# A two-layer encoder trunk on one core: attention by look-ahead, pooling maps by the half bank, and the output projection begun inside attention

## The chip, the cores and the metric

The kernel runs on one core of one Trainium2 chip. The time is the device time of one execution, in microseconds (us). The engines are PE (TensorE, matmuls and transposes), DVE (VectorE), ACT (ScalarE), POOL (GpSimd) and SP (SyncE, which here only issues DMAs). Each works through its own instructions in order and waits on semaphores for the others.

## The reference

Two layers over 528 tokens (16 meta tokens and 512 others) of width 1024, all in float32. Cut to what matters:

```python
for l in range(DEPTH):
    xn = rms_norm(h, attn_norm_g[l])
    q, k, v, u = jnp.split(xn @ w_in[l], splits, axis=-1)     # 512, 128, 128, 512 columns
    q = apply_rope(rms_norm(q, q_norm_g[l]), cos, sin) * q_scale
    k = apply_rope(rms_norm(k, k_norm_g[l]), cos, sin)
    attn = sliding_sink_attention(q, k, v, sinks[l])
    pool = multiscale_pool(u, w_pool[l], pool_scale[l])
    h = h + jnp.concatenate([attn, pool], axis=-1) @ w_out[l]
    xn = rms_norm(h, ffn_norm_g[l])
    g = causal_dwconv(xn @ w_gate[l], conv_w[l], conv_b[l])
    h = h + (gelu(g) * (xn @ w_up[l])) @ w_down[l]
```

There are 8 query heads and 2 key heads of 64. Attention goes by chunks of 64 queries; each sees the 16 meta tokens and its own and the previous chunk, with a learned sink in the softmax. The pooling mixer has four groups of 128 channels: the trailing mean over 2, 4, 8 or 16 positions less the token, and then a 128x128 map per group.

## The kernel before

Activations lie with features on the 128 partitions and the 528 tokens along the free dimension; a tile of the projection is 128 features by 528 tokens. PSUM holds it as a slot of two banks with 264 tokens in each (`slot[0..3]`). Every float32 product is made of three matmuls of rounded parts: weights high by activations high, high by low, low by high. So a tile over 1024 input features is 8 x 3 x 2 = 48 matmuls of 264 columns. ACT makes the high part of a weight block (`split_hi`, L391) and DVE the low part (`split_lo`, L404). A weight unit is 256 columns, and units take turns in two buffers; SP loads one when the low split of its predecessor in the buffer is done.

A layer's first half goes, on PE:

- the tiles k, v, the mean square of the features for the norm (its inverse root `rinv` is applied when a tile is evacuated), q0, the transposes of v, k's mean square, q1, q2, the means of q0 and q1 (`q_means`), q3, u3, five rows of the filling, the means of q2 and q3;
- eleven steps of attention. There are nine blocks b of queries (`NB`). Step s has `scores(s)`, `heads(s - 2)` and `probs_T(s - 1)` (the transposes of the probabilities). DVE in step s copies and evacuates `heads_lo(s - 3)`, divides block s - 1 by its sums (`divide`), takes the maxima of block s (`row_maxima`); ACT takes the exponentials of block s (`exps`), and copies;
- between them the filling (`project_side`): the pooling tiles u2, u1, u0 in half tiles of 264 tokens, in the one half bank that attention leaves free (`side`, in slot 3). One row is one input block: three matmuls. `SIDE_ENDS` says how many rows each step has in front of it in all. The half bank is free again when DVE's `u_half` has read it;
- the four pooling maps (`pool_map`, six matmuls each), over two banks of a slot of the scores, in the steps `MAP_AT`;
- the output projection, eight tiles of 48 matmuls, from the step after the last.

Rotary embedding is on three engines: DVE multiplies by the sines (`sine_part`), ACT shifts that by half a head (`shift`), POOL multiplies by the cosines and adds (`rotated`). POOL also makes the running sums of the pooling (`group`).

The order on each engine is written out by hand: the loop over steps stands once in each engine's block, with numbers of steps for what joins it. Each of the waits is a count of a semaphore: `filled[s]` and `evac[s]` for slot s (s = 4 is the side half bank), `hi_split` and `lo_split` for the weights, `meta_out` for DVE's copy of the meta probabilities, on which `heads` waits. In `split_hi` the count goes up only with the second half:

```python
            ins = nc.scalar.activation(w_hi[s][:, a:b], raw[s][:, a:b], ACT.Copy)
            if b == nk:
                ins.then_inc(hi_split[s], 1)
```

The MLP (from 177.3 us in layer 0 and 714.4 in layer 1) is computed in three chunks, with a fast scheme of seven products for the down projection. It has the same code before and after.

## Time and profile before

| | |
|---|---|
| median of 3 executions | 1091.09 us (1089.04 to 1093.24) |
| the profiled execution | 1094.96 us, span of its instructions 1093.2 us, granted clock 0.982 |
| PE busy | 1045.8 us (96%), 7932 matmuls |
| DVE busy | 738.5 us (68%) |
| ACT busy | 475.7 us (44%) |
| POOL busy | 107.7 us (10%) |
| HBM | 91.65 MB read, 86 GB/s over the span |

The ends of matmuls are modelled, and a busy PE is not PE at its peak: a matmul's row shows 280 ns at full clock while the next begins 120 ns after it. Busy time says little about the stages; what counts is when the first matmul of a stage starts, and what PE waited for. The first half of layer 0 lasts from 15.23 to 177.30 us, that of layer 1 from 561.66 to 714.45. The stages in them are: projections to 74.9 (615.6), steps to 129.3 (668.1), output projection.

### The profile page before, as it was taken

What the parts mean: (1) busy time and instruction counts of PE and PEld (TensorE: products, weight loads), DVE (VectorE), ACT (ScalarE), POOL (GpSimd) and SP (SyncE); (2) the same over time, 40 slices, a digit from 0 to 9 for tenths busy, and PEclk for the clock granted to TensorE, in tenths of its full rate; (3) what the DMA queues carried; (4) which work ended last, traced back from release to release, by engine and by line L of the source; (5) the groups of instructions that cost most, each with busy time, mean ns of one, the idle gap of its engine ahead of it and who ended that gap; (6) DMA issues with size and microseconds to landing.
All of it is one profiled execution on the core that took longest, in us unless ns stands there. A gap on an engine that the chain in (4) does not pass through costs nothing.

```text
span 1093.2 us, 19011 instructions
## 1 busy us (share of the span) xinstructions
PE 1045.8 (96%) x7932; PEld 999.3 (91%) x7932; DVE 738.5 (68%) x1134; ACT 475.7 (44%) x714; POOL 107.7 (10%) x109
## 2 busy tenths in 40 slices
PE   7899899999999999999899988999999999999997
PEld 6797799999999999999899977999989999899987
DVE  5566644568955689557886576546698466975686
ACT  5675534434413344134347755354343333423341
POOL 1262000000000000000002610001000000000000
PEclk9899899999999999999999999999999999999999
DMA  7211132232232322321231112332313332233112
GB/s 207 98 49 39 52 104 77 78 100 80 93 116 78 101 80 92 117 78 58 94 106 53 49 40 78 98 96 77 115 40 117 116 114 80 77 118 112 62 58 78
DMA packets 93566, 94.99 MB, mean 87 GB/s; under 512 B 3392, under 2 KB 91800, under 8 KB 93480
## 3 DMA queue, kind: packets, MB, share of 16 engines
q1 hardware_dynamic: 92768, 93.01, 26.5%
q8 instruction: 63, 1.03, 0.4%
q0 software_dynamic: 400, 0.58, 0.2%
q10 hardware_dynamic: 312, 0.18, 0.1%
q14 instruction: 23, 0.19, 0.1%
HBM read 91.65 MB, written 2.10 MB: 86 GB/s over the span
## 4 chain that ended last, share of the span: by engine, by line
PE 74%; DVE 12%; ACT 8%; issue 4%; DMA 1%; SPq 0%; POOL 0%; DVEq 0%; ACTq 0%; POOLq 0%
PE slot L552 57%; PE slot L787 14%; ACT probs L1065 3%; DVE h L1550 2%; ACT w_hi L400 1%; DVE nmax L1360 1%; DMA x_in<-in_x 1%; ACT rot_s L990 1%; DVE ms_work L1311 1%; DVE probs L1379 1%; DMA cst<-const_table 1%; ACT m_op_hi L1158 1%; DVE w_lo L411 1%; DVE mix_lo L1395 0%; ACT x_hi L917 0%
## 5 line engine op out<-in xcount | busy, mean ns | idle before, releaser
L552 PE MATMUL slot<-x_hi,w_hi 128*128 128x264 f32 (+2 forms) x1552 | 362.8, 301 | 7.0 <-DVE u_sb L1342 3.9
L552 PE MATMUL slot<-x_lo,w_hi 128*128 128x264 f32 (+2 forms) x1552 | 359.4, 299 | 0.0
L552 PE MATMUL slot<-x_hi,w_lo 128*128 128x264 f32 (+2 forms) x1552 | 359.0, 299 | 0.0
L552 PEld LDWEIGHTS slot<-x_hi,w_hi 128*128 128x128 f32 x1552 | 253.7, 190 | 19.6 <-DVE u_sb L1342 5.3
L552 PEld LDWEIGHTS slot<-x_lo,w_hi 128*128 128x128 f32 x1552 | 252.1, 190 | 7.3
L552 PEld LDWEIGHTS slot<-x_hi,w_lo 128*128 128x128 f32 x1552 | 251.9, 190 | 7.5
L411 DVE TENSOR_TENSOR w_lo<-raw,w_hi 128x2048 fp32r<-128x2048 f32 (+1 forms) x63 | 145.5, 2309 | 90.5 <-ACT w_hi L400 90.5
L400 ACT ACTIVATE w_hi<-raw 128x2048 fp32r<-128x2048 f32 (+2 forms) x65 | 118.3, 1820 | 145.2 <-PE slot L552 89.8
L903 POOL TENSOR_TENSOR work<-work 128x528 f32<-128x528 f32 (+1 forms) x32 | 41.9, 1309 | 714.0 <-DVE work L1481 350.6
L787 PE MATMUL slot<-m_op_hi,w_hi 128*128 128x264 f32 (+1 forms) x352 | 103.4, 294 | 8.3 <-DVE m_op_lo L1514 4.8
L787 PE MATMUL slot<-m_op_hi,w_lo 128*128 128x264 f32 (+1 forms) x352 | 100.9, 287 | 0.0
L787 PE MATMUL slot<-m_op_lo,w_hi 128*128 128x264 f32 (+1 forms) x352 | 100.9, 287 | 0.0
L1550 DVE TENSOR_TENSOR h<-slot,h 128x264 f32<-128x264 f32 (+1 forms) x192 | 79.5, 425 | 28.0 <-PE slot L787 24.1
L1135 ACT ACTIVATE work<-gate,par_all 128x528 f32<-128x528 f32 (+1 forms) x44 | 31.9, 731 | 118.6 <-DVE gate L1268 59.8
L438 ACT ACTIVATE w_hi<-w_sum 128x1024 fp32r<-128x1024 f32 (+1 forms) x48 | 47.4, 987 | 79.3 <-DVE w_sum L1532 60.7
L787 PEld LDWEIGHTS slot<-m_op_hi,w_hi 128*128 128x128 f32 x352 | 67.7, 192 | 12.5 <-DVE m_op_lo L1514 6.0
L787 PE MATMUL slot<-m_op_hi,w_ext_hi 128*128 128x264 f32 (+1 forms) x264 | 75.6, 286 | 1.8 <-DVE m_op_lo L1514 1.8
L787 PE MATMUL slot<-m_op_hi,w_ext_lo 128*128 128x264 f32 (+1 forms) x264 | 75.1, 285 | 0.0
L787 PE MATMUL slot<-m_op_lo,w_ext_hi 128*128 128x264 f32 (+1 forms) x264 | 75.0, 284 | 0.0
L787 PEld LDWEIGHTS slot<-m_op_lo,w_hi 128*128 128x128 f32 x352 | 67.8, 193 | 0.0
L787 PEld LDWEIGHTS slot<-m_op_hi,w_lo 128*128 128x128 f32 x352 | 67.8, 193 | 0.0
L1141 ACT ACTIVATE work<-work,par_all 128x528 f32<-128x528 f32 (+1 forms) x44 | 31.8, 730 | 70.6 <-DVE work L1472 70.4
(163 smaller groups left out, 1502.4 us busy)
## 6 DMA issues: line engine op xcount, KB each, us to landing
raw<-in_w_gate SPq DMA_DIRECT2D x44, 512.0 KB, 4.7
raw<-in_w_up SPq DMA_DIRECT2D x44, 512.0 KB, 4.6
raw<-in_w_down SPq DMA_DIRECT2D x32, 512.0 KB, 4.4
raw<-in_w_in SPq DMA_DIRECT2D x19, 512.0 KB, 5.0
raw<-in_w_out SPq DMA_DIRECT2D x16, 512.0 KB, 4.4
raw<-in_w_down SPq DMA_DIRECT2D x16, 384.0 KB, 3.6
x_in<-in_x SPq DMA_DIRECT2D x4, 512.0 KB, 6.3
out<-y_out SPq DMA_DIRECT2D x8, 256.0 KB, 2.9
```

Of the source, the lines that this page charges most:

```text
L400: ins = nc.scalar.activation(w_hi[s][:, a:b], raw[s][:, a:b], ACT.Copy)
L411: ins = nc.vector.tensor_tensor(w_lo[s][:, a:b], raw[s][:, a:b], w_hi[s][:, a:b].bitcast(f32), ALU.subtract)
L438: nc.scalar.activation(dst, src, ACT.Copy).then_inc(opnd_hi[n], 1)
L552: ins = nc.tensor.matmul(out_part, w[ws][:, r, cols], a[:, k, tokens], start=first and n == 0 and w is w_hi and a is a_hi, stop=end and w ...
L787: ins = nc.tensor.matmul(dst, part[s][w][:, wn, kk], m_op[a][:, m, kk, 0:width], start=first and kk == kks[0] and n == 0 and name in ("P1" ...
L903: nc.gpsimd.tensor_tensor(up[c][:, t0:], up[c][:, t0:], conv[c][:, t0:], ALU.mult)\
L990: ins = nc.scalar.activation(rot_s[to:to + 32], sine[fr:fr + 32], ACT.Copy)
L1065: ins = nc.scalar.activation(probs[:, y, t, 0:nk], slot[s][:, t // 2, col], ACT.Exp, bias=nm[:, y, t:t + 1], scale=q_scale[:, b, t // 2, t ...
L1135: nc.scalar.activation(conv[c][:, t0:], gate[c][:, 2 + t0:], ACT.Copy, scale=par[:, tap:tap + 1])\
L1141: nc.scalar.activation(conv[c][:, t0:], conv[c][:, t0:], ACT.Gelu, bias=par[:, bias:bias + 1])\
L1158: nc.scalar.activation(m_op[0][:, 3:7, kk, 0:width], m_sum[:, :, 0:width], ACT.Copy)\
L1550: nc.vector.tensor_tensor(rows, bank, rows, ALU.add).then_inc(h_added, 1)
```

## The change

- **Look-ahead.** `scores` and `row_maxima` run one step ahead of `exps`: PE makes `scores(s + 1)` and DVE `row_maxima(s + 1)` in step s. `scores(0)` and `row_maxima(0)` stand in front of the steps. The copy of the meta probabilities goes from the end of DVE's step to the head of the next.
- **Order of the tiles.** The units of w_in are cut anew (k with q3's columns, and so on, with the queries' tiles in reverse). k, norm, q0, k's mean, q1, q2, means, q3, u3, u0, means, `scores(0)`, and then v, whose transposes are in step 1. u3 and u0 are whole tiles in front; u2 and u1 are the filling, 32 rows in steps 1 to 4.
- **Maps.** One map in each of the steps 5 to 8, in two halves of three matmuls through the side half bank; ACT and DVE evacuate each half (264 columns) in place of 528.
- **Output projection.** `out_rows` makes the four pooling rows of tile out0 in step 9 and of out1 in step 10; the attention rows follow by halves of the tokens. Splits of w_out are made in halves in steps 6 to 11.
- **Rotary.** `sine`, `rot_c` and `rot_s` are doubled, in memory of v_T and of the running sums, so that a stage waits for the tile before last.
- **First norm of layer 0.** Row sums of squares come from ACT (`accum_out`) on x before its transposes, with a root and a reciprocal of [128, 5]; five small matmuls spread them over the partitions. The layer's squares, their sums, the logarithm and the exponential go. ACT copies the result to `rinv` and loads the table of roots at the start.
- **Constants.** The table of sines, cosines and counts is loaded by SP, after the first weights, and no longer by POOL after the sinks.

The diff, cut to its core:

```diff
@@ Psum: order of the slots
-            order += [(f"scores{b}", 1 - b % 2)] + {5: [("pool3", 1)], 8: [("pool2", 0), ("pool1", 0)]}.get(b, [])
+        order += [(f"scores{b}", b % 2) for b in range(NB)]
+        order += [(f"{name}{half}", 4) for name in ("u2", "u1", "pool3", "pool0", "pool2", "pool1") for half in "ab"]
...
-            sine = v_T[:]
+            sine = [v_T[:], run_b[:, PAD:]]
+            rot_c = [sb(sc, f"rot_c{n}", [P, L])[:] for n in range(2)]
+            rot_s = [sb(sc, "rot_s", [P, L])[:], run_a[:, PAD:]]
...
-        GROUPS = (3, 2, 1, 0)
-        SIDE_ENDS = [5, 8, 14, 20, 26, 32, 38, 44, 48, 48, 48, 48, 48]
-        POOLED_AT, POOL_HI_AT, POOL_LO_AT, MAP_AT = (1, 4, 6, 9), (2, 5, 7, 9), (3, 6, 9, 9), (5, 8, 9, 10)
+        GROUPS = (3, 0, 2, 1)
+        SIDE_ENDS = [0, 0, 8, 16, 24, 32, 32, 32, 32, 32, 32, 32, 32]
+        POOLED_AT, POOL_HI_AT, POOL_LO_AT, MAP_AT = (0, 1, 4, 5), (1, 2, 6, 7), (2, 3, 6, 7), (5, 6, 7, 8)
...
@@ PE
-                for step in range(NB + 2):
-                    if step < NB:
-                        scores(step)
+                scores(0)
+                project("v", U_VU0)
+                for step in range(NB + 2):
+                    if step == 1:
+                        v_transposed()
...
+                    project_side(first, cut)
+                    if step + 1 < NB:
+                        scores(step + 1)
+                    if step == NB:
+                        open_slot("out0", l)
+                        pe.wait_ge(lo_split[U_OUT % 2], slot_turn(l, U_OUT) + 2)
+                        out_rows(0, (7, 4, 6), first=True)
+                    if step == NB + 1:
+                        open_slot("out1", l)
+                        out_rows(1, (7, 4, 6, 5), first=True)
                     if step >= 2:
                         heads(step - 2)
+                    if step in MAP_AT:
+                        pool_map(MAP_AT.index(step), 0)
+                    if step == NB:
+                        out_rows(0, (5,))
                     if 1 <= step <= NB:
                         probs_T(step - 1)
+                    if step in MAP_AT:
+                        pool_map(MAP_AT.index(step), 1)
                     project_side(cut, end)
...
@@ ACT
+                act.wait_ge(x_loaded[t], 16)
+                nc.scalar.activation(y_out[:, t], x_in[:, t], ACT.Square, accum_out=row_ms[:, t:t + 1])\
+                  .then_inc(row_summed, 1)
...
-            for k in range(KT):
-                square(0, 0, k)
...
+                    if step in MAP_AT:
+                        for half in range(2):
+                            pool_map_hi(MAP_AT.index(step), half)
+                    if step in POOL_HI_AT:
+                        pooled_hi(POOL_HI_AT.index(step))
+                    if step in (6, 7):
+                        split_hi(act, l, U_OUT, half=step - 6)
+                    if step in (9, 10):
+                        split_hi(act, l, U_OUT + 1, half=step - 9)
@@ DVE
                     if 3 <= step < NB + 2:
                         meta_probs_out(step - 2)
                     if step >= 3:
                         heads_lo(step - 3)
                     if 1 <= step <= NB:
                         divide(step - 1)
-                    if step < NB:
-                        row_maxima(step)
+                    if step + 1 < NB:
+                        row_maxima(step + 1)
                     if side_done(step) is not None:
                         u_half(side_done(step))
+                    if step in MAP_AT:
+                        for half in range(2):
+                            pool_map_lo(MAP_AT.index(step), half)
+                    if step in (7, 8):
+                        split_lo(dve, l, U_OUT, half=step - 7)
+                    if step in (9, 11):
+                        split_lo(dve, l, U_OUT + 1, half=step // 2 - 4)
```

PE's order at a map, in layer 0. Before (step 5 with the third pooling group's map over both banks of slot 1; `pool_hi` is the pooled tile, `x_hi` the filling, `k_win` the scores, `v_meta` the heads, `probs_pad` the transposes):

```order
L669 MATMUL slot0<-k_win,q_rot 128x144 x3
L552 MATMUL slot1<-pool_hi,w_hi1 128x264 [waits plo_ready,lo_split1,evac1]
L552 MATMUL slot1<-pool_hi,w_hi1 128x264
L552 MATMUL slot1<-pool_lo,w_hi1 128x264 x2
L552 MATMUL slot1<-pool_hi,w_lo1 128x264 x2
L552 MATMUL slot3<-x_hi,w_hi0 128x264 [waits evac4]
```

and after, the same step:

```order
L697 MATMUL slot0<-k_win,q_rot 128x144 x3
L724 MATMUL slot3<-probs_meta,v_meta 128x128 [waits meta_out,evac2,evac3]
L724 MATMUL slot3<-probs_meta,v_meta 128x128
L731 MATMUL slot3<-probs_win,v_win 64x128 x4
L569 MATMUL slot3<-pool_hi,w_hi1 128x264 [waits plo_ready,lo_split1,evac4]
L569 MATMUL slot3<-pool_lo,w_hi1 128x264
L569 MATMUL slot3<-pool_hi,w_lo1 128x264
L709 MATMUL slot2<-cst,probs_pad 128x128 [waits probs_ready,meta_out,evac2]
L712 MATMUL slot2<-cst,probs 128x128 x4
L569 MATMUL slot3<-pool_hi,w_hi1 128x264 [waits plo_ready,evac4]
L569 MATMUL slot3<-pool_lo,w_hi1 128x264
L569 MATMUL slot3<-pool_hi,w_lo1 128x264
```

The map went from one group of six, with its own slot and filling behind it, to two groups of three in the half bank, the second of which waits for `evac4`, the evacuation of the first.

DVE's order behind the row maxima of layer 0. Before, in step 6 (`u_sb` is the evacuation of the half bank):

```order
L1365 TENSOR_TENSOR sink_arg<-nm,sink_all 128x4 [waits dve_attn]
L1342 TENSOR_TENSOR u_sb<-slot3,rinv 128x264 [waits filled4,pooled_ready]
L1294 SCALAR_TENSOR_TENSOR pooled<-run_a,u_sb 128x528 [waits plo_ready,run_ready]
L1300 TENSOR_TENSOR pool_lo<-pooled,pool_hi 128x528 [waits phi_ready]
L1388 COPY probs_meta<-slot2 128x128 [waits filled2]
L1395 TENSOR_TENSOR mix_lo<-slot3,mix_hi 128x4x64 [waits mixhi_ready]
```

and after, in step 7 (`mix_lo` from `par_all` is a map's half, `w_lo0` the first half of the low split of w_out):

```order
L1416 TENSOR_TENSOR sink_arg<-nm,sink_all 128x4 [waits dve_attn]
L1400 SCALAR_TENSOR_TENSOR mix_lo<-slot3,par_all,mix_hi 128x264 [waits mixhi_ready] x2
L1352 TENSOR_TENSOR pool_lo<-pooled,pool_hi 128x528 [waits phi_ready]
L421 TENSOR_TENSOR w_lo0<-raw0,w_hi0 128x1024 [waits hi_split0]
L1439 COPY probs_meta<-slot2 128x128 [waits filled2]
L1446 TENSOR_TENSOR mix_lo<-slot3,mix_hi 128x4x64 [waits mixhi_ready]
```

Both halves of the map and the split now stand ahead of the copy and the heads' `mix_lo`, which PE's next heads wait for (`meta_out`, `evac3`).

## Rows read from the trace of the kernel before

**Rows 1.** windows: length, busy us (x) of PE PEld DVE ACT POOL, PEclk, DMA

```profile
15.20:74.90 59.70, 54.33 (x403) 53.31 (x404) 37.26 (x39) 44.40 (x68) 20.00 (x22) 0.91 0.27 82
74.90:97.80 22.90, 20.84 (x167) 18.13 (x167) 15.38 (x47) 11.76 (x47) 7.99 (x9) 0.93 0.04 12
97.80:129.30 31.50, 25.35 (x202) 20.86 (x202) 24.06 (x62) 20.02 (x65) 3.96 (x5) 0.93 0.12 38
129.30:177.30 48.00, 48.00 (x387) 48.00 (x385) 21.80 (x23) 16.49 (x19) 0.00 (x0) 0.97 0.34 108
561.70:615.60 53.90, 51.94 (x404) 50.86 (x403) 33.19 (x33) 37.62 (x56) 18.73 (x19) 0.97 0.26 83
638.00:668.10 30.10, 23.95 (x203) 19.54 (x202) 23.75 (x62) 20.03 (x65) 3.97 (x5) 1.00 0.11 36
668.10:714.40 46.30, 46.30 (x384) 46.30 (x385) 21.94 (x24) 16.49 (x19) 0.00 (x0) 1.00 0.36 114
```

**Rows 2.** waits of PE: who waited for whom, us in total, times, longest us

```profile
PE slot L696 <- DVE mix_lo L1395: 6.5, 8, 1.2
PE slot L621 <- DVE v_T L1268: 4.6, 2, 3.9
...
PE slot L552 <- DVE u_sb L1342: 3.9, 6, 1.1
```

**Rows 3.** windows over three stretches at half clock

```profile
15.90:19.30 3.40, 3.40 (x18) 3.40 (x17) 3.40 (x6) 3.40 (x6) 0.60 (x1) 0.50 0.06 0
39.80:46.60 6.80, 5.85 (x23) 5.39 (x24) 2.12 (x4) 5.70 (x12) 1.30 (x1) 0.50 0.40 139
125.10:131.90 6.80, 6.26 (x30) 5.71 (x31) 3.87 (x5) 2.71 (x3) 0.00 (x0) 0.50 0.46 152
```

**Rows 4.** timeline of PE: start us, us, operation, count, [idle before <-releaser]

```profile
57.00 2.07 PE L607 MATMUL slot<-cst,head_sq 128*128 128x2 f32 x18
...
95.81 0.29 PE L552 MATMUL slot<-x_hi,w_lo 128*128 128x264 f32 x1
95.93 0.61 PE L696 MATMUL slot<-probs_meta,v_meta 128*128 128x128 f32 x4
...
97.06 0.33 PE L681 MATMUL slot<-cst,probs_pad 128*128 128x128 f32 x1
...
97.75 0.76 PE L669 MATMUL slot<-k_win,q_rot 64*128 64x144 f32 x8
```

**Rows 5.** timeline of DVE, a split in front and a step of attention

```profile
19.75 1.22 DVE L1242 TENSOR_TENSOR w_lo<-raw,w_hi 128x1024 fp32r<-128x1024 f32 x1
...
94.50 0.42 DVE L1395 TENSOR_TENSOR mix_lo<-slot,mix_hi 128x256 fp32r<-128x256 f32 x1 [1.71 <-ACT mix_hi L1086]
94.84 0.15 DVE L1371 TENSOR_TENSOR den<-row_sum,sink_exp 128x4 f32<-128x4 f32 x1
...
95.99 0.75 DVE L1360 TENSOR_REDUCE nmax<-slot 128x4 f32<-128x576 f32 x1
...
97.25 0.43 DVE L1342 TENSOR_TENSOR u_sb<-slot,rinv 128x264 f32<-128x264 f32 x1
```

**Rows 6.** waits of ACT before 16 us

```profile
ACT h L939 <- PE slot L586: 4.5, 4, 2.1
```

**Rows 7.** timeline of ACT

```profile
18.41 1.04 ACT L947 ACTIVATE w_hi<-raw 128x1024 fp32r<-128x1024 f32 x1
...
33.36 1.92 ACT L400 ACTIVATE w_hi<-raw 128x2048 fp32r<-128x2048 f32 x1 [4.62 <-DMA cst<-const_table]
35.30 1.28 ACT L963 ACT_TABLE_LOAD   x1
...
99.27 0.38 ACT L1086 ACTIVATE mix_hi<-slot 128x256 fp32r<-128x256 f32 x1
```

**Rows 8.** timeline of POOL and DVE at 88 us

```profile
88.20 1.07 POOL L884 TENSOR_TENSOR run_a<-run_b 128x528 f32<-128x528 f32 x1
...
88.36 0.93 DVE L1371 TENSOR_TENSOR den<-row_sum,sink_exp 128x4 f32<-128x4 f32 x1
```

More of the change, by code:

```diff
@@ L530, in open_slot, with dense @@
                 return s
-            def dense(s, ws, col, rows, a_hi, a_lo, first=True, last=True, ready=None, part=None, real=False, tail=False):
+            def dense(s, ws, col, rows, a_hi, a_lo, first=True, last=True, ready=None, part=None, real=False, tail=False,
+                      parts=(0, 1)):
                 if real:
@@ L622, in _ @@
-                nc.tensor.transpose(flat[0:N_META, NWIN * P:(NWIN + 1) * P], v_T[:, 0:N_META], ident)\
-                  .then_inc(filled[s], 1)
+                project("k", U_KQ3, ready=lambda k: pe.wait_ge(xlo_ready, l * (2 * KT) + (k + 1)))
+                if l > 0:
+                    column_mean("attn_norm", l, all_mean, sumsq, *norm_added(l, 0, KT - 1))
+                else:
+                    s = open_slot("attn_norm", 0)
+                    pe.wait_ge(row_inv, 1)
+                    for t, (bank, c0, n) in enumerate(ROW_TILES):
+                        ins = nc.tensor.matmul(slot[s][:, bank, c0:c0 + n], row_ms[0:n, t:t + 1].broadcast_to([n, P]),
+                                               ident[0:n, 0:n], start=True, stop=True)
+                    ins.then_inc(filled[s], 1)
@@ new lines, in _, with v_transposed @@
+                project("u3", U_Q0U3)
+                project("u0", U_VU0)
+                q_means(1)
+                def v_transposed():
+                    s = open_slot("v_T", l)
+                    pe.wait_ge(evac[ps.slot("v")], ps.before("v", l) + 1)
+                    flat = slot[s][:].rearrange("p a t -> p (a t)")
+                    for w in range(NWIN):
+                        t0 = N_META + w * CHUNK
+                        nc.tensor.transpose(flat[:, w * P:(w + 1) * P], v_T[:, t0:t0 + P], ident)
+                    nc.tensor.transpose(flat[0:N_META, NWIN * P:(NWIN + 1) * P], v_T[:, 0:N_META], ident)\
+                      .then_inc(filled[s], 1)
@@ L706, in heads @@
                     ins.then_inc(filled[s], 1)
-                name = "heads0"
-                pe.wait_ge(evac[ps.slot(name)], ps.before(name, l))
-                project_side(*side_rows(-1))
-                q_means(1)
-                for step in range(NB + 2):
-                    if step < NB:
-                        scores(step)
-                    for n in (0, 1):
-                        if step == MAP_AT[n]:
-                            pool_map(n)
-                    first, end = side_rows(step)
-                    done = side_done(step)
-                    cut = (first + end) // 2 if done is None else (done + 1) * KT
-                    project_side(first, min(cut, end))
+                last_layer = l + 1 == DEPTH
@@ new lines, in out_rows @@
+                def out_rows(t, ks, first=False, last=False, parts=(0, 1)):
+                    s, unit = ps.slot(f"out{t}"), U_OUT + t // 2
+                    for k in ks:
+                        if k >= 4:
+                            name = f"pool{k - 4}b"
+                            pe.wait_ge(evac[4], ps.before(name, l) + 1)
+                    return dense(s, unit % 2, (t % 2) * P, [(k, k) for k in ks], mix_hi, mix_lo, first=first, last=last,
+                                 tail=last_layer, parts=parts)
@@ L749, in _ @@
-                for t in range(KT):
-                    s, unit = open_slot(f"out{t}", l), U_OUT + t // 2
+                for t in range(2):
+                    out_rows(t, (0, 1, 2, 3), last=True, parts=(0,))
+                name = f"heads{NB - 1}"
+                pe.wait_ge(evac[ps.slot(name)], ps.before(name, l) + 1)
+                for t in range(2):
+                    out_rows(t, (0, 1, 2, 3), last=True, parts=(1,)).then_inc(filled[ps.slot(f"out{t}")], 1)
+                for t in range(2, KT):
+                    s, unit = open_slot(f"out{t}", l), U_OUT + t // 2
+                    if t == 2:
+                        pe.wait_ge(meta_out, l * (NB - 1) + (NB - 1))
@@ L751, in _ @@
                     if t % 2 == 0:
                         pe.wait_ge(lo_split[unit % 2], slot_turn(l, unit) + 2)
-                    dense(s, unit % 2, (t % 2) * P, rows, mix_hi, mix_lo, ready=mixed if t == 0 else None,
-                          tail=l + 1 == DEPTH).then_inc(filled[s], 1)
+                    out_rows(t, (7, 4, 6, 5, 0, 1, 2, 3), first=True, last=True).then_inc(filled[s], 1)
                 def mlp_tiles(i):
@@ L1304, in _ @@
                 scaled("k", k_dup[:, 0])
-                scaled("v", v_T[:])
                 q_tile(0)
                 dve.wait_ge(qtab_ready, l + 1)
-                dve.wait_ge(evac[ps.slot("v_T")], ps.before("v_T", l) + 1)
                 sine_part(0)
```

347 lines of the change are left out of this document (166 added, 181 removed).

## The prediction

> **What bounds the kernel now.** I read the windows by stage first [rows 1]. TensorE (PE) is busy almost throughout, and the out projection shows its bare speed: 384 matmuls of 264 columns in 48.0 us, less the slow clock at its start, 0.122 us each, so 48 of them (a tile) take 5.86 us, and with the switch of operand ahead of it about 5.96. The attention block of a layer, from the first scores to the out projection, takes 54.4 us in layer 0 (22.9 and 31.5) and 52.5 in layer 1. Its matmuls, by the spacing of one step [rows 4] (heads 1.13, transposes of the probabilities 0.69, scores 0.7), are 43 side rows of three (15.7), four maps (2.9), scores 6.1, heads 9.5, transposes 5.6, together 39.8 us; so 13 to 15 us in each layer are waits and slow clock. The list of PE's waits [rows 2] names what ends them: mix_lo (the evacuation of the heads' bank), u_sb (of the side half bank), and ahead of attention v_T, 3.9 us of it in layer 0. Third, the granted clock: after the wait on v_T it was half for 6.8 us (0.50, that is 1.2 GHz), as at the very start for 3.4 us, and again at the end of layer 0's steps [rows 3]. Fourth, one step of attention on PE, DVE and ACT [rows 4, 5]: PE goes from heads to the next scores in 1.8 us and then has the side rows or a map; DVE works in strict order: heads' low part, division, row maxima, side half bank, and what else the step has.
>
> **Front of layer 0.** Five squares with a row sum join ACT ahead of the copies of h, each about 1.1 us (1024 columns took 1.04), 5.5 us; ACT waited 4.5 us for PE there, so 1.1 us come late, with the small root [rows 6]. The first matmul goes from 15.2 to 16.3. In return eight squares, seven sums, and two table loads of 1.28 leave the path to rinv, and so does ACT's wait for the constant table (4.6 us of waiting at 33.4) [rows 7]. From there PE: seven tiles (k, four q, u3, u0) 41.7, norm 1.1, k's mean square 0.7, two means of q 2.0 each [rows 4], 1.7 for the slow clock at the start, and a new wait of 1.1: k's squares follow, on ACT and DVE, the copies of rinv, a split of 1.9, one of 2.3 and k_dup. Sum 50.3: the first scores come at 66.6. Before: 59.7 us with 5 side rows (1.8) and the transposes of v (0.9) more, so 57.0 against 50.3, a gain of 6.7, less 1.1 for the late start. The double rot_c, rot_s and sine take POOL and ACT off each other's way, but no longer wait of PE names them in the old trace [rows 2]: nothing, and the least of it is shown by the 2 us by which my places for the low splits lie ahead of the tiles that need them. The const load stands on SP's queue behind the first weights and in front of the next ones; those land 1.5 us later and are used 8 us later: nothing.
>
> **Front of layer 1.** The old order has 53.9 us, the wait on v_T and one on head_sq in it; the same work less 5 side rows and v's transposes would be 51.2. The new: seven tiles 41.7, about 0.5 for x_lo's pace, norm 0.7, k's mean 0.7, means of q 4.0, sum 47.6, so the scores start at 609.3. Gain 3.6.
>
> **Steps 0 to 4.** v's tile fills the time in which the first scores go through DVE and ACT: 0.55 and 5.96. Then scores 0.7, 0.25 waiting for v_T, transposes 0.9, four steps with 8 side rows (2.93 and 0.2 for switches) 12.5, scores 2.8, heads 2.8, transposes 2.2. Between two half tiles PE waits for u_sb: the last matmul's 0.28, DVE 0.43 [rows 4, 5], 0.13 to restart, less the usual spacing, 0.74, three times 2.2. Sum 24.3; v done at 73.1, the side rows at 97.4 (layer 1: 640.1). The exponentials do leave the loop, as the order shows: row maxima run a step ahead. In units of the old work this part is 1.4 us quicker in layer 0, about 1 in layer 1.
>
> **Steps 5 to 8** carry the loss. Side rows are gone, and each step has one map in two halves through one half bank, in the order heads, map a, transposes, map b; DVE takes both evacuations one after the other, and only after them, at the head of the next step, the copy of the meta probabilities and mix_lo, on which PE's heads wait. From the start D of DVE's step: copy 0.2, mix_lo 0.34 and 0.08, PE restarts at 0.75, heads to 1.88, map a to 2.35, drained 2.51; ACT's half 0.40 (256 columns took 0.38 [rows 7]) to 2.95; DVE is then just through with the division (1.15) and the maxima (1.26); its half 0.42 to 3.4; map b 3.6 to 4.2 drained; ACT 4.66; DVE 5.07. Then a pooled tile 0.61 (step 5), or ACT's 0.65 and DVE's 0.61 (step 6): periods 5.7 and 5.85 for 3.6 us of PE work. Step 7: ACT's half split of w_out (1.04) in step 6 delays its heads by 0.5, and at its end DVE's first half of the low split waits for ACT's second half, since the semaphore is counted only at the whole: 7.85. Step 8: 5.07 and another half split of 1.22 [rows 5], and PE opens out0 at 6.4. D5 is at 99.15 (97.4, then u_sb, pooled, split), D6 105.65, D7 111.5, D8 119.35. One collision with POOL is in D6: the last tile's adds run in step 5, and DVE's 4-column sum took 0.93 instead of 0.15 beside such an add [rows 8]; 0.8.
>
> The Trainium skill (SBUF — State Buffer, section Who interferes with whom) says that a VectorE instruction with two SBUF inputs is blocked for the whole of a GpSimd instruction that reads SBUF. The rows agree for one add: both ended at 89.3. By the rule both adds of the last tile can block one DVE instruction each, 2.1 us in place of 0.8, which would make the time 2.6 us longer in the two layers.
>
> Step 9 and 10: eight rows of out0 and out1 (5.86 and switches 0.3) stand between the last heads, 7 to 10 us of work that was behind them. DVE's half split in step 9 waits for ACT's step 10 and costs 0.6 ahead of heads8, done at D8 + 16.25 = 135.6. The remaining out rows take 41.1: end at 176.7, before 177.3. Layer 1: 640.1 + 38.2 + 40.2 = 718.6 (the last layer's tiles are narrower), before 714.4.
>
> **Clock.** In step 7 to 8 PE stands for 4.0 us, and waits of 1.5 to 2.4 stand in each step. In the old trace a wait of 3.9 was followed by 6.8 us at half clock, and smaller ones, 0.8 to 1.2 each, by 6.8 us at the end of layer 0 and by none in layer 1 [rows 1, 3]. A stretch of 3.4 us costs up to 1.7. No such stretch per layer is one end and three the other, 0 to 5.1 us; I take 2.5, one and a half of them, nearest to the row of the 3.9 us wait (two, with much of the first spent idle).
>
> **Sum.** −0.6 and +4.2 and 2 × 2.5 = +8.6 us. MLP, load sizes and the end are unchanged. The profiled execution (span 1093.2, time 1094.96) would be 1103.5; it is 3.9 above the median of 1091.09, so the median becomes 1099.6.
>
> **Rivals.** (A) *Faster, 1084, chance 0.20*: the half-bank trips of steps 5 to 8 fit beside PE's other work. I price the late stretch 7 us a layer above the old one in like work (38.2 with 6.1 of out rows, against 31.5 with 5.9 of side rows); if it costs no more than before, the sum without clock is +3.6 − 14 = −10, with some clock −7. It decides when PE's waits in steps 5 to 8 fall below 7 us a layer; I work out 14. For it: half of them hang on ACT's and DVE's order being as tight as I add it. Against: the waits on mix_lo are there today, with fewer trips.
> (B) *No change, 1093, chance 0.27*: the clock holds through the steps and POOL does not collide: 3.6 − 1.6 = +2. For it: layer 1 of the old kernel had no slow stretch in these steps.
> (C) *The head start doesn't come, 1106, chance 0.07*: the sinks, landed at 26 us before, land later; ACT now waits for them (through DVE's preparation) ahead of k's squares. Seven us later and layer 0's gain is gone.
> The forecast: 0.46.
>
> A difference under 0.5% (5.5 us) is about what this measurement can't tell from none. Faster than that: A, 0.20. Within: B with 0.27 and 0.03 of the forecast's own low side, 0.30. Slower: 0.43 and C, 0.50. Range 1083 to 1107; the forecast's own, by the clock's bounds (−5 to +5.2) and 2.6 of POOL, 1094 to 1107.
>
> **What would show it.** Right: first matmul near 16.3, no wait on v_T above 0.5, scores0 at 66 to 67; PE waits on mix_lo of 1.5 to 2.5 in four steps and 4.0 in one, one on w_lo near 2 ahead of out0; half clock at step 8; layer 0's out projection ends at 177 to 180, layer 1's stage grows from 152.8 to 157 to 160 us. Wrong: periods of steps 5 to 8 under 5 us, or a front of layer 0 that is not 5 us shorter.

## The result, and the profile after

The changed kernel takes 1111.5 us, median of 4 runs (1108.3 to 1113.6), against 1090.5 (1089.0 to 1093.2) of the kernel before: ratio 1.0187, 95% interval 1.0164 to 1.0210. It is slower, as forecast, but by 21 us where I had 8.6, and outside the range of 1083 to 1107. Its profiled execution took 1111.45 us with a span of 1109.7, 16.5 more than the span before.

The windows by stage of the changed kernel, in the columns of [rows 1]: the front, first scores to the filling's end, then to the end of the last heads, the out projection; in layer 1 the front, steps 5 to the last heads, out projection; and two stretches at half clock:

```profile
17.95:67.86 49.91, 49.15 (x387) 48.67 (x387) 33.68 (x31) 31.05 (x49) 24.61 (x25) 0.97 0.24 70
67.86:100.25 32.39, 30.32 (x245) 27.52 (x244) 20.04 (x53) 19.50 (x68) 5.58 (x6) 0.95 0.11 34
100.25:144.68 44.43, 31.32 (x194) 25.54 (x193) 24.33 (x61) 19.60 (x57) 3.13 (x3) 0.77 0.15 48
144.68:185.65 40.97, 40.97 (x339) 40.97 (x337) 20.29 (x23) 14.37 (x18) 0.00 (x0) 1.00 0.32 104
568.41:616.12 47.71, 47.33 (x382) 46.63 (x380) 34.09 (x32) 34.07 (x49) 23.55 (x23) 1.00 0.25 73
647.02:690.87 43.85, 30.22 (x194) 24.72 (x194) 24.32 (x61) 19.60 (x57) 3.13 (x3) 0.81 0.15 49
690.87:731.55 40.68, 40.68 (x338) 40.68 (x337) 20.21 (x23) 14.38 (x18) 0.00 (x0) 1.00 0.32 104
124.30:131.10 6.80, 5.07 (x23) 4.07 (x23) 3.21 (x8) 3.01 (x12) 0.00 (x0) 0.50 0.00 0
670.40:677.20 6.80, 4.90 (x22) 3.95 (x23) 3.33 (x8) 3.17 (x13) 0.00 (x0) 0.50 0.00 0
```

In layer 0 the front is 49.9 us where it was 59.7 [rows 1], or 57.0 in like work; the filling's end to the last heads takes 44.4, and in layer 1 43.9, where the prediction had 38.2. Of these 44 us PE is busy for 31, and its mean clock is 0.77 and 0.81. The rest of the out projection takes 41.0 and 40.7, close to the forecast of 41.1 and 40.2. PE's waits (us in total, times, longest), to be held against [rows 2]:

```profile
PE slot L724 <- DVE mix_lo L1446: 14.5, 8, 3.8
...
PE slot L569 <- issue: 4.6, 2, 2.3
PE slot L724 <- ACT probs_win L1131: 4.3, 2, 2.2
...
PE slot L655 <- DVE v_T L1318: 0.7, 2, 0.4
```

The wait on mix_lo ahead of the heads went from 6.5 to 14.5 us with one of 3.8; that on v_T, 3.9 before, is two of 0.36. "issue" is the wait for out0's weights, 2.3 us a layer. How a step comes to its wait is seen at the head of step 7 of layer 1. ACT first:

```profile
660.72 0.48 ACT L1058 ACTIVATE mix_hi<-slot,par_all 128x264 fp32r<-128x264 f32 x1 [1.35 <-PE slot L569]
661.10 0.63 ACT L1053 ACTIVATE pool_hi<-pooled 128x528 fp32r<-128x528 f32 x1
661.63 1.04 ACT L410 ACTIVATE w_hi<-raw 128x1024 fp32r<-128x1024 f32 x1
662.58 0.37 ACT L1141 ACTIVATE mix_hi<-slot 128x256 fp32r<-128x256 f32 x1
662.85 0.59 ACT L1131 ACTIVATE probs_win<-slot 128x512 f32<-128x512 f32 x1
```

then DVE, and PE, whose heads wait at 661.4 (scores behind half b, and the idle time in brackets):

```profile
661.24 0.49 DVE L1400 SCALAR_TENSOR_TENSOR mix_lo<-slot,par_all,mix_hi 128x264 fp32r<-128x264 f32 x1 [1.34 <-ACT mix_hi L1058]
661.77 0.71 DVE L1352 TENSOR_TENSOR pool_lo<-pooled,pool_hi 128x528 fp32r<-128x528 f32 x1
662.39 0.28 DVE L1439 COPY probs_meta<-slot 128x128 f32<-128x128 f32 x1
662.99 0.42 DVE L1446 TENSOR_TENSOR mix_lo<-slot,mix_hi 128x256 fp32r<-128x256 f32 x1 [0.31 <-ACT mix_hi L1141]
```

```profile
660.61 0.76 PE L697 MATMUL slot<-k_win,q_rot 64*128 64x144 f32 x8
663.54 1.15 PE L724 MATMUL slot<-probs_meta,v_meta 128*128 128x128 f32 x4 [2.16 <-ACT probs_win L1131]
```

The heads of the step before had been finished at 657.8, yet ACT touches them (L1141) at 662.58: ahead stand half b of step 6's map (660.72), which PE makes only after half a was read out, the pooled tile and a half split. DVE's copy of the meta probabilities (L1439) and mix_lo (L1446) stand behind the same half b, and PE's new heads wait 2.16 us for both engines.

One side term can be read at once. POOL's last sum runs in step 5 of layer 0; POOL, and the two instructions of DVE that end with its two adds:

```profile
101.55 1.38 POOL L923 TENSOR_TENSOR run_b<-u_sb 128x528 f32<-128x528 f32 x1 [8.89 <-DVE pooled L1346]
103.01 1.07 POOL L923 TENSOR_TENSOR run_a<-run_b 128x528 f32<-128x528 f32 x1
```

```profile
102.46 0.49 DVE L1422 TENSOR_TENSOR den<-row_sum,sink_exp 128x4 f32<-128x4 f32 x1
...
103.20 0.96 DVE L1426 TENSOR_TENSOR probs_pad<-probs,rden 128x64 f32<-128x64 f32 x1
```

They take 0.49 and 0.96 where they take 0.15 ([rows 5]) and 0.23 (at 656.39 us in the next step of layer 1) elsewhere: 1.07 us together, and the same in layer 1. The prediction had 0.8 a layer from one collision [rows 8]. The Trainium skill (SBUF — State Buffer, section Who interferes with whom) was right that both adds hold one DVE instruction each; the 2.1 us that I had worked out from it for that are twice the measured cost. Each instruction is held only for what is left of its add when it begins, 0.47 us of the first and 0.88 of the second, and would itself have taken 0.15 and 0.23 of that.

### The profile page after: what moved, and what is told of

The parts are those of the page before. It is cut to its first block, busy times and chain, and to the rows that moved or that the text cites. A ratio compares the mean times of both kernels' runs of the same rounds, so it can differ in the third digit from the quotient of the medians.

```text
span 1109.7 us, 19066 instructions
## 1 busy us (share of the span) xinstructions
PE 1050.9 (95%) x7938; PEld 1002.0 (90%) x7938; DVE 743.3 (67%) x1139; ACT 474.8 (43%) x725; POOL 111.3 (10%) x108
## 4 chain that ended last, share of the span: by engine, by line
PE 84%; DVE 8%; issue 4%; ACT 2%; DMA 1%; SPq 0%; DVEq 0%; ACTq 0%
PE slot L569 65%; PE slot L826 14%; DVE h L1600 2%; PE slot L724 1%; PE slot L731 1%; DMA x_in<-in_x 1%; DVE w_lo L421 1%; ACT w_hi L410 1%; PE slot L623 1%; PE slot L712 1%; PE slot L697 1%; ACT m_op_hi L1209 1%; DVE w_sum L1580 0%; PE slot L579 0%; DVE x_lo L1277 0%
## 5 line engine op out<-in xcount | busy, mean ns | idle before, releaser
L569 PE MATMUL slot<-x_hi,w_hi 128*128 128x264 f32 (+2 forms) x1552 | 357.9, 299 | 6.6 <-DVE u_sb L1394 3.4
L569 PE MATMUL slot<-x_lo,w_hi 128*128 128x264 f32 (+2 forms) x1552 | 355.4, 298 | 0.0
L569 PE MATMUL slot<-x_hi,w_lo 128*128 128x264 f32 (+2 forms) x1552 | 355.3, 298 | 0.0
L569 PEld LDWEIGHTS slot<-x_lo,w_hi 128*128 128x128 f32 x1552 | 249.6, 189 | 7.3
L421 DVE TENSOR_TENSOR w_lo<-raw,w_hi 128x2048 fp32r<-128x2048 f32 (+2 forms) x67 | 148.2, 2212 | 94.1 <-ACT w_hi L410 94.1
L1186 ACT ACTIVATE work<-gate,par_all 128x528 f32<-128x528 f32 (+1 forms) x44 | 31.9, 730 | 118.7 <-DVE gate L1318 59.9
L826 PEld LDWEIGHTS slot<-m_op_hi,w_hi 128*128 128x128 f32 x352 | 66.2, 188 | 14.5 <-issue 7.6
```

Source lines behind the costliest of these rows:

```text
L421: ins = nc.vector.tensor_tensor(w_lo[s][:, a:b], raw[s][:, a:b], w_hi[s][:, a:b].bitcast(f32), ALU.subtract)
L569: ins = nc.tensor.matmul(out_part, w[ws][:, r, cols], a[:, k, tokens], start=first and n == 0 and w is w_hi and a is a_hi, stop=end and w ...
L826: ins = nc.tensor.matmul(dst, part[s][w][:, wn, kk], m_op[a][:, m, kk, 0:width], start=first and kk == kks[0] and n == 0 and name in ("P1" ...
L1186: nc.scalar.activation(conv[c][:, t0:], gate[c][:, 2 + t0:], ACT.Copy, scale=par[:, tap:tap + 1])\
```

## The experiments

In each pair of numbers the first is layer 0. "Late stretch" is from the end of the filling to the end of the last heads. Ratios are to the kernel before, which ran beside each.

**e1: PE kept busy in its waits.** In the changed kernel:

```diff
+                FILLER = {5: 10, 6: 10, 7: 14, 8: 26, 9: 16}
...
+                        filler(FILLER.get(step, 0), open_slot(f"scores{step + 1}", l))
                         scores(step + 1)
+                    if step == NB - 1:
+                        filler(FILLER.get(step, 0), open_slot("out0", l))
                     if step == NB:
-                        open_slot("out0", l)
+                        filler(FILLER.get(step, 0), open_slot("out0", l))
```

`filler(n, s)` issues n matmuls of x_hi by x_hi, 264 columns, into the slot just opened, which the next real matmul overwrites.

> The changed kernel with 76 more matmuls a layer whose result is thrown away, of 264 columns each, put into the waits of PE that its trace shows (10, 10, 14, 26 and 16 of them in steps 5 to 9, ahead of the scores or of out0). No other instruction changes. Theory CLOCK (the 17 to 20 us a layer at half clock make the stretch from the filling's end to heads8, 44.4 and 43.9 us, longer than the 38.2 worked out at full clock): the granted clock stays at 1.0 there, both stretches shrink to 38.5 to 40 us, and the time falls by 8 to 11 us, ratio 0.990 to 0.993. Rival STRUCTURE (the waits on ACT and DVE set the periods and the slow clock only fills what would be waits): clock at 1.0 as well, but stretches within 1 us of 44, ratio 1.000.

Measured: 1101.5 us (1.0099, 1.0077 to 1.0122), 10 us less than the changed kernel. The late stretches (windows):

```profile
100.71:139.22 38.51, 32.85 (x271) 28.31 (x269) 24.31 (x61) 19.69 (x57) 3.13 (x3) 1.00 0.17 56
643.62:682.09 38.47, 32.86 (x271) 28.29 (x270) 24.30 (x61) 19.68 (x57) 3.13 (x3) 1.00 0.17 56
```

38.5 and 38.5 us at full clock, against 38.2 worked out. So the structure was priced right within 0.3 us a layer, and the half clock cost 5.9 and 5.4 us a layer there: theory CLOCK. More work on PE made the kernel faster.

**e2: half b read out late.** ACT and DVE serve the next step's heads first:

```diff
 # ACT                                     # DVE in the same way, with meta_probs_out, heads_lo, pool_map_lo
                     if 2 <= step < NB + 2:
                         probs_out(step - 2)
+                    if step - 1 in MAP_AT:
+                        pool_map_hi(MAP_AT.index(step - 1), 1)
                     if step < NB:
                         exps(step)
                     if step in MAP_AT:
-                        for half in range(2):
-                            pool_map_hi(MAP_AT.index(step), half)
+                        pool_map_hi(MAP_AT.index(step), 0)
```

> The changed kernel with the second half of each map read out later: ACT and DVE first do the next step's copies and low part of the heads, and then half b of the map. PE's order is the same. Theory TRIPS (heads wait because both halves of a map stand ahead of the copy of the meta probabilities and of mix_lo): PE's waits on mix_lo in steps 6 to 9, 1.6, 2.2, 3.8 and 2.3 us, shrink by 1.5 to 2 us each, the stretch from the filling's end to heads8 goes from 44 to 36 to 39 us, the clock has fewer slow windows, time 12 to 18 us shorter, ratio 0.984 to 0.989. Rival CHAIN (exponentials, division and transposes set the period): under 3 us in all, ratio above 0.997.

Measured: 1091.2 us (1.0004, 0.9989 to 1.0020): the whole of the 20 us is back, more than I expected. The late stretches:

```profile
98.15:130.00 31.85, 23.71 (x194) 19.16 (x193) 23.67 (x61) 19.37 (x57) 3.13 (x3) 1.00 0.21 67
634.56:668.37 33.81, 26.55 (x194) 21.75 (x194) 23.73 (x61) 19.47 (x57) 3.14 (x3) 0.90 0.19 63
```

31.9 us at full clock in layer 0 (and 6.8 us at half clock in layer 1's): 6.6 less than e1 has. ACT at the same place as above:

```profile
645.80 0.38 ACT L1141 ACTIVATE mix_hi<-slot 128x256 fp32r<-128x256 f32 x1
646.06 0.60 ACT L1131 ACTIVATE probs_win<-slot 128x512 f32<-128x512 f32 x1
646.54 0.49 ACT L1058 ACTIVATE mix_hi<-slot,par_all 128x264 fp32r<-128x264 f32 x1
```

The high part of the heads and probs_win now come ahead of half b (646.54), and of the waits of 1.6 and 2.2 us ahead of the heads of steps 6 and 7 nothing is left; of the 3.8 in step 8, 1.65 is left, and the 1.58 of step 5 stays. The two late stretches are 12.6 and 10.0 us shorter than in the changed kernel, and 6.7 and 4.7 shorter than in e1. So about half of the gain is the order itself, and the other half is half clock that doesn't come up any more. Theory TRIPS, though "trips" is not the right word, as e9 shows.

**e3: DVE's half split counted by itself** (a semaphore `half_split` that ACT's first half raises, and DVE's first half waits for in place of `hi_split`).

> The changed kernel with one more semaphore: ACT counts the first half of its split of w_out, and DVE's first half waits for that alone. Theory SPLIT WAIT (DVE's half split in step 7 waits for ACT's second half ahead of the heads, and in step 9 for that of step 10): 0.2 to 0.5 us a layer in step 7, where the trace of the changed kernel shows only 0.24 us of DVE waiting, and 0 to 0.6 in step 9; time 0.5 to 2 us shorter, ratio 0.998 to 0.9995. Rival, as the prediction had it (7.85 against 5.85 us for step 7, the split wait its larger part): 2 us a layer, ratio 0.996.

Measured: 1109.8 us (1.0175, 1.0150 to 1.0199), 1.7 us off. The runs spread from 1107.8 to 1112.0, those of the changed kernel from 1108.3 to 1113.6, so a small gain can't be told from none; the rival's 4 us are at the edge of the interval. In the prediction's step 7 the wait was meant to cost more. That step's 7.85 us held all the same: at full clock, in e1, DVE's copies of the meta probabilities of steps 7 and 8 of layer 1 start at 658.12 and 666.01, 7.89 us apart. What is in them besides the wait, the split itself and ACT's, was not separated.

**e4: no head start.** `out_rows` of steps 9 and 10 and the half splits go; ACT splits w_out at step 9, DVE at step 10, the rows follow the steps.

> The changed kernel without the output projection in steps 9 and 10 and without the half splits of w_out in steps 6 to 11: the splits are whole, at step 9 (ACT) and 10 (DVE) and after the steps, and all rows of out0 and out1 follow the steps. Theory TRIPS: DVE and ACT lose 1.2 and 1.0 us in each of the steps 6 to 8, so the stretch to heads8 shrinks by 3 for these and by 7 for the rows of out0 and out1 that are made later, while the rows come after it with a wait for the splits of 2 to 4 us: time within 3 us of the changed kernel. Rival HEAD START PAYS: steps 9 and 10 stand empty for about 6 us a layer, 8 to 12 us slower, ratio above 1.007.

Measured: 1111.5 us (1.0190, 1.0167 to 1.0212), no change, as TRIPS had it. But one of its windows shows what else is in it:

```profile
114.50:138.40 23.90, 18.69 (x85) 14.66 (x86) 11.72 (x31) 12.59 (x31) 0.00 (x0) 0.50 0.05 13
```

23.9 us in one piece at half clock in layer 0's late steps. Without the rows of out0 and out1 in them these steps keep PE less busy, so the comparison holds the clock too; e11 makes it again.

**e5: late half b, the semaphore of e3, and 24 fillers a layer** (10 in step 5, 10 in step 8, 4 in step 9).

> The kernel with half b read out late, with the half split's own semaphore, and with 24 thrown-away matmuls a layer in the waits of PE that its trace still shows (10 in step 5, 10 in step 8, 4 in step 9). The run of half b late had 3.4 and 10.2 us at half clock in the two layers' steps and took 1091.2. Theory CLOCK: with the filling the second layer's 6.8 us at half clock in steps 8 and 9 go, and its steps, 65.0 us from the first scores, come down to the first layer's 63.0; with 0.5 to 1 us a layer from the semaphore the time is 1087 to 1089, ratio to the kernel before 0.997 to 0.999. Rival STRUCTURE: nothing but the semaphore's part, 1089.5 to 1091.

Measured: 1086.8 us (0.9973, 0.9960 to 0.9985), below both kernels. No half clock is left in the steps of layer 0, and in layer 1 only 3.4 us right behind the first scores. This is read from the trace of an execution of 1084.85 us, 2.0 under the median.

**e6: ACT's part of e2 alone** (DVE still reads half b ahead of the copy and mix_lo).

> The changed kernel with ACT's part of the late reading alone: ACT makes the next step's copies (high part of the heads, probabilities) before the high part of half b, while DVE still has the low part of half b ahead of the copy of the meta probabilities and of mix_lo. Theory DVE ORDER (DVE's strict order is what holds the heads): as half b's low part now waits for an ACT that is 0.8 us later with it, heads come later still or the same: time within 4 us of the changed kernel's 1111.5. Rival ACT ORDER (the copies on ACT were late, the heads waited for probs_win and mix_hi): at least half of the 20 us gained by the late reading come back here, 1095 to 1102.

Measured: 1099.5 us (1.0087, 1.0074 to 1.0100): 12 of the 20 us. I had named DVE's order as the cause; ACT's was the larger part.

**e7: the kernel before, with fillers in the wait on v_T** (28 matmuls behind `open_slot("v_T", l)` in layer 0).

> The kernel before with 28 thrown-away matmuls in layer 0's wait of PE for v_T (3.9 us long), in the bank that v's transposes use next; nothing else. Its trace shows 6.8 us at half clock behind that wait, in which transposes, the mean square and q1's start take 16.0 us instead of 13.4. Theory CLOCK: full clock behind the wait, 2.0 to 2.8 us faster, ratio 0.9975 to 0.998. Rival: the slow clock comes from something else than the wait and stays, ratio 1.000.

Measured: 1094.1 us (1.0037, 1.0023 to 1.0051), slower: a miss for both. The clock behind the wait did come back (first row). But a stretch of 6.8 us at half clock stands at 74.9 (second row), where the first trace of the kernel before had one of 3.4 at 80.8:

```profile
39.80:46.60 6.80, 6.80 (x56) 6.65 (x55) 1.24 (x2) 4.26 (x9) 1.33 (x1) 1.00 0.27 92
74.90:81.70 6.80, 6.05 (x33) 5.67 (x34) 3.86 (x11) 3.00 (x11) 5.29 (x6) 0.50 0.25 84
```

**e8: DVE's half splits of w_out moved** to just ahead of the low part of half a, on top of e5.

> The kernel of the late half b, semaphore and filling, with DVE's two half splits of w_out in steps 7 and 8 moved from the step's end to just before the low part of the map's half a, where DVE waits for ACT 1.4 and 2.7 us in the trace of the changed kernel. Theory TRIPS: the wait on mix_lo in step 8 (1.65 us) and the one on w_lo before out0 (0.55) go and about 2 us a layer are won, time 1083 to 1086. Rival: half a's low part comes up to 1.2 us later, so map b and the step after it do as well, and nothing is won: within 1 us of the kernel without the move.

Measured: 1087.7 us (0.9978, 0.9966 to 0.9990), nothing won. DVE in step 7 of layer 1, and PE's half b behind it:

```profile
653.98 1.22 DVE L427 TENSOR_TENSOR w_lo<-raw,w_hi 128x1024 fp32r<-128x1024 f32 x1
655.11 0.49 DVE L1417 SCALAR_TENSOR_TENSOR mix_lo<-slot,par_all,mix_hi 128x264 fp32r<-128x264 f32 x1
```

```profile
655.65 0.39 PE L575 MATMUL slot<-pool_hi,w_hi 128*128 128x264 f32 x1 [1.96 <-DVE mix_lo L1417]
```

The rival: the split pushes half a's low part to 655.11, and half b waits 1.96 us for it. (The trace is of an execution of 1092.48 us, 4.8 over the median; the order on the engines is the same in all.)

**e9: half b in a place of its own.** `side_b = slot[2][:, 1, P:P + HALF]` with a semaphore pair of its own.

> The changed kernel with half b of each map in a place of its own (the unused 264 columns of the bank of the meta probabilities), so that PE makes half b without waiting for the evacuation of half a; ACT's and DVE's orders are as in the changed kernel. Theory ORDER (what costs is the order in which ACT and DVE serve the halves, not the one place in PSUM): PE's waits ahead of half b, 0.83 us in one step and under 0.4 in the others, go and come back in the wait ahead of the heads; 0 to 4 us off the 1111.5. Rival PING-PONG (the one half bank sets the period, as the prediction put it): 10 us or more off, as with the late reading.

Measured: 1103.7 us (1.0119, 1.0097 to 1.0141), 7.8 us off, between the two theories. PE's waits:

```profile
PE slot L726 <- DVE mix_lo L1448: 15.0, 8, 3.8
...
PE slot L571 <- issue: 4.6, 2, 2.3
```

The wait ahead of the heads is 15.0 us, 0.5 more than in the changed kernel, and the separate place is worth far less than the 20 us of the late reading: theory ORDER as to the mechanism, though the size is above its range. From the first scores to the last heads the trace has 73.4 and 74.4 us against 76.8 and 74.8, so 3.8 us come from there, and 2.0 of the span from an earlier first matmul (15.96 against 17.95), together the 5.8 by which the spans differ. The median fell by 2 us more, since this trace is of an execution 2.0 us above its median. How much of the 7.8 us is the separate place, and how much is the start and the clock, stays open.

**e10: DVE's part of e2 alone.**

> The changed kernel with DVE's part of the late reading alone: DVE makes the next step's copy and the heads' low part before the low part of half b, while ACT still makes half b's high part before the heads' high part and probs_win. ACT's part alone gave 12 us of the 20. Theory ADD: DVE's part alone gives little, since the heads' low part still waits for ACT behind half b: 1108 to 1112. Rival: each part alone gives more than half (both stand in the same loop): 1098 to 1103.

Measured: 1102.8 us (1.0116, 1.0092 to 1.0139): 8.7 us, more than my theory gave, and in the rival's range, though not the half that it asks for. With ACT's 12.0 the parts add up to 20.7, about the 20.3 of e2: each engine's order was a cost of its own.

**e11: late half b, fillers in steps 5 and 8, no head start** (e4's edit on e2).

> The kernel of the late half b with 20 thrown-away matmuls a layer (steps 5 and 8) and without the output projection and w_out's half splits inside the steps (whole splits at step 9 and 10, all rows of out0 and out1 behind the steps). In the changed kernel the same removal left the time where it was (1111.5), with 28.5 us at half clock in layer 0's late steps in place of 24. With half b late the loop is shorter. Theory HEAD START PAYS now that the loop is short: steps 9 and 10 stand empty 4 to 6 us a layer against 1 to 2 of split work taken out of steps 6 to 8: 5 to 10 us slower than the 1087 to 1091 with it, 1093 to 1099. Rival NEUTRAL: within 2 us of 1089.

Measured: 1091.7 us (1.0012, 0.9999 to 1.0026). Against 1091.2 (e2) and 1086.8 (e5) the head start is worth between nothing and 5 us (e5 also has the semaphore and four more fillers a layer); the steps 9 and 10 that stand empty cost little more than the splits in steps 6 to 8 did. Nearer to NEUTRAL than to the 5 to 10 us that I expected.

**e12: the next scores between transposes and half b in steps 5 and 6**, on top of e5.

> The kernel of the late half b with semaphore and filling, and in steps 5 and 6 the next step's scores made between the transposes and half b of the map, where its trace shows PE waiting 0.83 us for half a's low part. Theory GAP: the 0.69 us of scores fit into that wait, twice a layer, 2 to 3 us off the 1086.8, ratio to the kernel before 0.994 to 0.996. Rival LOOP: the steps are bound by the loop over half a, half b and the heads on ACT and DVE, PE then waits as much longer ahead of the heads: 1086 to 1088.

Measured: 1085.2 us (0.9945, 0.9927 to 0.9964), the fastest version; its interval overlaps with that of e5. The late stretch of layer 0 in e5 and in e12, and PE's heads in step 7 of layer 1 of e12:

```profile
97.55:128.72 31.17, 26.48 (x220) 21.98 (x218) 23.67 (x61) 19.48 (x57) 3.13 (x3) 1.00 0.22 69
```

```profile
97.61:128.67 31.06, 26.65 (x219) 21.97 (x217) 23.68 (x61) 19.46 (x57) 3.14 (x3) 1.00 0.22 69
```

```profile
645.45 0.68 PE L730 MATMUL slot<-probs_meta,v_meta 128*128 128x128 f32 x4 [0.69 <-ACT probs_win L1149]
```

The windows differ by 0.1 us, and the gap has turned into a wait of 0.69 on ACT's probs_win: the LOOP over ACT and DVE binds, not PE. That this version's median is 1.6 us lower is not explained by its steps: the two traces have the same span, 1083.1 us.

**e13 and e14: the kernel before, and the same with e7's filling, once more.**

> The kernel before, unchanged, in one more profiled execution. It tells how far its own places of half clock and its first matmul (15.2 us in the first trace) move between executions. If they are a property of the kernel: slow stretches at 16, 40, 81 and 125 us and the first matmul within 0.3 us of 15.2. If they belong to the execution: the first matmul between 15 and 18 with the landing of the second load of x (6.8 to 8.3 us), and the slow stretches moved or gone.

> The kernel before with 28 thrown-away matmuls in the wait on v_T once more. In the first run the stretch at half clock behind the wait was gone, and one of 6.8 us stood at 74.9 instead of 3.4 us at 80.8; the time was 3.8 us longer. If the filling itself pushes the slow stretch behind the means of q2 and q3 (74.9), it stands there again; if that was chance, it does not. If the 3.8 us came from a late start of this execution, the first matmul is now near 15.5 and the time near 1091.

Measured: 1089.3 and 1093.3 us, one execution each. The first one's front of layer 0 and its stretch at half clock, its wait on v_T, and the second one's longest stretch at half clock in layer 0:

```profile
17.43:72.79 55.36, 51.64 (x403) 50.75 (x404) 37.59 (x40) 44.88 (x69) 19.99 (x22) 1.00 0.28 88
75.00:81.80 6.80, 5.91 (x33) 5.46 (x31) 3.96 (x15) 3.56 (x19) 2.49 (x3) 0.50 0.00 0
```

```profile
39.56 0.96 PE L621 MATMUL slot<-cst,v_T 128*128 128x128 f32 x7 [0.56 <-DVE v_T L1268]
```

```profile
58.40:65.20 6.80, 6.80 (x32) 6.80 (x32) 6.25 (x6) 5.20 (x9) 4.21 (x4) 0.50 0.08 25
```

In e13 the stretches at 16, 40 and 125 us of [rows 3] are gone, and one that stood at 81 stands at 75 and is twice as long; the front takes 55.4 us in place of 59.7, and the first matmul comes at 17.4, not 15.2. So both belong to the execution. In e14 it is q3's and u3's tiles that run at half clock. And the wait on v_T is 0.56 us in e13, where it was 3.9 in the trace that I read: PE comes to it 2.2 us later (at 39.0), and v_T is ready 1.2 us earlier. In such an execution 28 fillers (3.4 us) stand in almost no wait. The transposes of v start at 42.43 in e7 and at 39.56 in e13, so 2.9 us of the 3 to 4 that e7 and e14 lose are the fillers themselves.

The place of the first matmul can be followed further back. Ahead of it stand the transposes of x; these are the last 16 in the first trace of the kernel before, and then in the changed kernel:

```profile
10.14 1.09 PE L586 MATMUL slot<-cst,x_in 128*128 128x128 f32 x8 [0.72 <-DMA x_in<-in_x]
11.45 1.09 PE L586 MATMUL slot<-cst,x_in 128*128 128x128 f32 x8 [0.22 <-DMA x_in<-in_x]
```

```profile
11.52 3.67 PE L603 MATMUL slot<-cst,x_in 128*128 128x128 f32 x16 [0.19 <-DMA x_in<-in_x]
```

The same 16 transposes take 2.2 us in one and 3.7 in the other. Of the sixteen traces (four of the kernel before and its versions, twelve of the changed one and its versions) seven have 2.2 us there and the first matmul at 15.2 to 16.3; the other nine, e13 among them, have 3.3 to 3.7 us and the first matmul at 16.8 to 18.5. The windows show a clock of 1.00 in both, so what makes the transposes longer stays open.

## Why the prediction was wrong

Direction and place were right, the size was not. Point by point:

- *Front of layer 0*, 50.3 from first matmul to first scores: 49.9. Front of layer 1, 47.6: 47.7. v's end to the end of the filling, 24.3: 24.3.
- *The baseline of that gain* was off. I held 50.3 against 57.0 to 59.7 of one execution, in which 6.8 us at half clock and a wait on v_T of 3.9 stood in the front. In e13 the old front is 55.4, or 52.7 in like work. A gain of 6.7 was thus for the larger part one of the clock and of that wait, which e13 does not pay: the old half of layer 0 takes 155.3 us in e13 and 162.1 in the first trace. The shift of 3.9 us between that execution and the median covered part of it.
- *First matmul*, 16.3: between 15.9 and 18.5 in twelve traces of the changed kernel and its versions, and 15.2 to 17.6 in four of the kernel before. Most of this spread goes with the transposes of x. Where they are quick, it is 15.9 to 16.3 in six traces with the change and 15.2 in the one without; where they take longer, 16.8 to 18.5 and 17.0 to 17.6. So 1.1 us is possible, but not shown. The forecast started from a trace of the quick kind, and the changed kernel's trace is of the other.
- *v's tile*, 5.96: 7.56, with 3.4 us at half clock right behind the means of q and the first scores. Not foreseen; 1.6 us in layer 0.
- *Steps 5 to 8*, the late stretch of 38.2: 38.5 at full clock (e1), and of the 0.3 above it POOL's two adds, 1.07 us for 0.8, may make nearly all. The waits ahead of the heads were forecast as 1.5 to 2.5 in four steps and 4.0 in one, with one near 2 ahead of out0: in layer 0 they are 1.58, 1.11, 2.17 and 3.84, and 2.28. But the cause was put down wrongly in part. The trips through one half bank are worth 7.8 us at most (e9), the count of `hi_split` hardly shows (e3), and it is not DVE's order alone: ACT served half b before finished heads, and that was 12 of the 20 us (e6, e2).
- **The step that failed is the clock**, "0 to 5.1 us; I take 2.5" a layer. In the trace the late steps have 20.4 and 17.0 us at half clock, where I had taken 5; they cost 5.9 and 5.4 us a layer in the late stretch and 1.6 in v's tile, 12.9 in all where the sum has 5. The bound came from the old kernel, where waits of 1 to 4 us were followed by 6.8 us of it at most [rows 3]. Here the waits repeat in five steps in a row with 4 to 5 us of PE work between, and each slow stretch lengthens the matmuls that sit in the loop, on which ACT and DVE wait. I had worked out 14 us of PE waits a layer and priced the clock as if they were the old 7.
- *Sum*. Trace against trace the span grew by 16.5 us, 7.9 more than the 8.6 forecast, and the clock's 12.9 in place of 5 are 7.9 of it. The other terms cancel: the late first matmul and small items add 2.2, and the two MLPs are 2.2 shorter than in the old trace. The remaining 4.5 of the 12.4 us by which I missed the medians' difference come from the baseline: the execution that I read, 1094.96 us, lay 4.4 above the kernel's median of 1090.5, while that of the changed kernel lay at its own. I had subtracted 3.9 for this from both kernels alike. So the agreement of "structure" with its forecast holds against that one trace only. The spans of e13 (little half clock, the kernel before), e1 (the changed one at full clock in its late stretches) and the changed kernel are 1087.4, 1100.8 and 1109.7: held against e13, the change costs some 13 us by its structure, start included, and 9 by the clock.
- *Rivals*: A (half-bank trips fit beside PE's work) is what e2 comes near to by reordering: its late stretch of layer 0, 31.9 us, is about the old one's 31.5, though the time is 1091.2 and not 1084. B needed the clock to hold; with it held in the late stretches (e1) the time is 1101.5, not 1093. C didn't occur.

## What to carry to other kernels

When PE's waits repeat in every one of a row of short steps, price the slow clock for the whole row at half clock as the upper end, not by single waits of an older trace; a version with thrown-away matmuls in the waits separates clock from structure in one run (here 10 of 21 us). On ACT and DVE try the work that PE waits for ahead of work that PE has only just made: reordering two read-outs there, without touching PE's order, gave 20 us. And read two executions of the baseline before counting a gain against a stretch of it that ran at half clock or stood in a long wait.

## What the runs showed of the hardware

- The place of the half clock moves between executions of one kernel where its waits are few (16, 40, 81 and 125 us in one, 75 in the other), while in the one trace of the changed kernel both layers had 17 to 20 us of it in steps 5 to 9, and e4 23.9 in one piece. Thrown-away matmuls in the waits removed it (clock 1.00 in both late stretches of e1).
- Fillers paid where the wait was there in every trace read, and cost time where it was not: 24 a layer in e5 gave 4 us together with the semaphore, 28 in the kernel before, in a wait of 3.9 us in one execution and 0.56 in another, took 3 to 4.
- The first matmul of one kernel moved by 2.2 us between two executions (15.2 and 17.4). The last 16 transposes of x ahead of it took 2.2 us in the one and 3.7 in the other, and all sixteen traces fall into these two kinds.
